# Weight-part stores moved from SyncE's queue to GpSimd's, and the weight-sum batches regrouped from 5, 6, 5 to 4, 6, 6

## What is computed

```
for l in range(DEPTH):
    h = _rmsnorm(x, norm_gain[l])
    proj = jnp.einsum('bsd,de->bse', h, w_in[l])               # 2048 x 4352
    q, k, v, g_attn, x_rnn, g_rnn = jnp.split(proj, splits, axis=-1)
    attn = _swa_sink_attention(q, k, v, sinks[l], cos, sin)
    xc = _causal_conv(x_rnn, conv_w[l], conv_b[l])
    rnn = _rg_lru(xc, w_rgate[l], b_rgate[l], w_igate[l], b_igate[l], lru_param[l])
    mixed = jnp.concatenate([attn * silu(g_attn), rnn * silu(g_rnn)], axis=-1)
    x = x + jnp.einsum('bse,ed->bsd', mixed, w_out[l])         # 2048 x 2048
return _rmsnorm(x, final_gain)
```

## Time and profile before

| | value |
|---|---|
| median of three runs | 2289.14 us |
| profiled execution | 2285.01 us, its span 2283.2 us |
| PE busy | 2275.7 us (100%) |
| DVE / ACT busy | 1568.7 us (69%) / 1315.0 us (58%) |
| POOL busy | 84.9 us (4%) |
| SP's queue q1 | 381.56 MB, 52.4% of the 16 DMA engines' span |
| POOL's queue q0 | 62.92 MB, 11.4% |
| HBM | 222 GB/s over the span |

### The profile page before, as it was taken

The page is one execution under the profiler, slowest core; times in us unless marked ns, Lnnn a source line. Parts: engine busy times, 40 slices in busy tenths (PEclk is TensorE's granted clock), DMA queues, the critical chain, the costliest instruction groups (busy, mean ns, idle before and its releaser), DMA issues.

```text
span 2283.2 us, 38210 instructions
## 1 busy us (share of the span) xinstructions
PE 2275.7 (100%) x14446; PEld 1939.6 (85%) x14446; DVE 1568.7 (69%) x2594; ACT 1315.0 (58%) x2536; POOL 84.9 (4%) x138
## 2 busy tenths in 40 slices
PE   9999999999999999999999999999999999999998
PEld 7888888899888888889988888888988888888898
DVE  7658778656546876856677777785568468778555
ACT  7558666444455867645565575663446557566444
POOL 1110000000111000000011100000000000000000
PEclk9999999999999999999999999999999999999999
DMA  8987777544788777644479866654545346666444
GB/s 255 258 234 259 238 241 239 156 135 142 212 245 233 252 235 240 214 142 138 139 233 267 263 206 203 214 190 146 141 130 170 99 134 196 208 202 196 140 134 153
DMA packets 173271, 447.01 MB, mean 196 GB/s; under 512 B 20768, under 2 KB 25120, under 8 KB 167200
## 3 DMA queue, kind: packets, MB, share of 16 engines
q1 hardware_dynamic: 165744, 381.56, 52.4%
q0 software_dynamic: 6912, 62.92, 11.4%
q10 hardware_dynamic: 432, 0.10, 0.0%
HBM read 365.85 MB, written 141.56 MB: 222 GB/s over the span
## 4 chain that ended last, share of the span: by engine, by line
PE 98%; DMA 1%; DVE 0%; ACT 0%; issue 0%; POOL 0%; ACTq 0%; DVEq 0%; POOLq 0%
PE proj L719 74%; PE proj L740 18%; PE ps_at L848 2%; PE ps_at L823 1%; PE ps_at L867 1%; PE proj L759 1%; DMA wall<-in_w 1%; PE proj L786 0%; ACT wcut L942 0%; PE ps_at L674 0%; DVE acc L1439 0%; ACT operand L979 0%; PE ps_at L801 0%; ACT sqr L1005 0%; DVE operand L1416 0%
## 5 line engine op out<-in xcount | busy, mean ns | idle before, releaser
L719 PE MATMUL proj<-operand,wcut 128*128 128x512 f32 x7512 | 1745.2, 391 | 0.3 <-DVE operand L1416 0.3
L719 PEld LDWEIGHTS proj<-operand,wcut 128*128 128x128 f32 x7512 | 1400.0, 188 | 297.4 <-issue 9.6
L1344 DVE TENSOR_TENSOR wcut<-wall,wcut 128x512 fp32r<-128x512 f32 x799 | 550.1, 688 | 537.1 <-ACT wcut L942 530.5
L942 ACT ACTIVATE wcut<-wall 128x512 fp32r<-128x512 f32 x798 | 501.9, 629 | 596.9 <-DMA wall<-in_w 322.8
L740 PEld LDWEIGHTS proj<-operand,wcut 128*128 128x128 f32 x1476 | 187.8, 191 | 6.5
L740 PE MATMUL proj<-operand,wcut 128*128 128x256 f32 x1476 | 189.8, 283 | 0.0
L740 PE MATMUL proj<-xsum_out,wcut 128*128 128x256 f32 x1104 | 136.8, 283 | 0.0
L740 PEld LDWEIGHTS proj<-xsum_out,wcut 128*128 128x128 f32 x1104 | 134.9, 192 | 0.6
L740 PE MATMUL proj<-xsum_in,wcut 128*128 128x256 f32 x864 | 111.8, 284 | 0.0
L740 PEld LDWEIGHTS proj<-xsum_in,wcut 128*128 128x128 f32 x864 | 107.9, 191 | 3.5 <-issue 1.7
L1048 ACT ACTIVATE gy<-proj 32x512 f32<-32x512 f32 x144 | 85.0, 590 | 14.9 <-PE proj L719 9.5
(11 more groups left out here) (186 smaller groups left out, 1733.6 us busy)
## 6 DMA issues: line engine op xcount, KB each, us to landing
wall<-in_w SPq DMA_DIRECT2D x494, 256.0 KB, 2.8
weight_cuts<-wcut SPq DMA_DIRECT2D x126, 512.0 KB, 3.9
wcut<-weight_cuts SPq DMA_DIRECT2D x126, 512.0 KB, 4.2
weight_sums<-in_blocks POOLq DMA_DIRECT2D x84, 512.0 KB, 6.6
wall<-weight_sums SPq DMA_DIRECT2D x164, 256.0 KB, 2.7
wall<-in_blocks SPq DMA_DIRECT2D x141, 256.0 KB, 2.8
weight_sums<-weight_sums POOLq DMA_DIRECT2D x28, 512.0 KB, 5.0
x<-in_xt SPq DMA_DIRECT2D x16, 512.0 KB, 3.7
```

The source lines that it names most:

```text
L719: last = pe.matmul(bank_of(l, 2 * g + m)[:, :], wcut[:, n % RING, a, c:c + P], operand[:, k, b, :], start=(i == 0 and k == 0), stop=(k == ...
L942: act.activation(wcut[:, u % RING, 0, :], wall[:, u % RING, 1, :], ACT.Copy).then_inc(w_hi, 1)
L1344: dve.tensor_tensor(wcut[:, u % RING, 1, :], wall[:, u % RING, 1, :], wcut[:, u % RING, 0, :].bitcast(F32), ALU.subtract).then_inc(w_lo, 1)
```

## The change

The 126 stores leave SP's loop. POOL issues them, 63 at a time, in a new function `store_parts(l)`: for each stored unit of layer l it waits on `w_lo` and issues the same 512 KB store. It calls this at the two turns of `OPENS`, after the closing addition of S4 and before the wait for PE. `OPENS` moves one turn forward: batches 0 to 3 come first, then the stores of layer 0; from unit 220 batches 4 to 9, then the stores of layer 1; from slot 4 of (h 1, l 0) batches 10 to 15.

```diff
-OPENS = {5: (0, 1, 1), 11: (1, 0, 4)}
+OPENS = {4: (0, 1, 1), 10: (1, 0, 4)}
...
                                 w_load(u + RING)
-                            if u + 2 in STORED:
-
-                                sp_.wait_ge(w_lo, SPLIT_NO[u + 2])
-                                sp_.dma_start(cuts[KEYS.index(key_of(l, *UNIT[u + 2][2:]))],
-                                              wcut[:, (u + 2) % RING, :, :].rearrange("p a c -> p (a c)").bitcast(F32)
-                                              ).then_inc(cut_out[(u + 2) % RING], 16)
...
+            def store_parts(l):
+
+                for n in STORED:
+                    if UNIT[n][1] == l:
+                        pool.wait_ge(w_lo, SPLIT_NO[n])
+                        pool.dma_start(cuts[KEYS.index(key_of(*UNIT[n][1:]))],
+                                       wcut[:, n % RING, :, :].rearrange("p a c -> p (a c)").bitcast(F32)
+                                       ).then_inc(cut_out[n % RING], 16)
+
             pool.wait_ge(unit_done, START_SUMS)
...
                 if n in OPENS:
                     pool.wait_ge(built[S4], 32 * n - 16)
                     add(S4, n - 1, A12)
+                    store_parts(list(OPENS).index(n))
                     pool.wait_ge(unit_done, at_unit(*OPENS[n]))
```

## The result

The changed kernel takes 2314.8 us, the median of five runs (2313.8 to 2317.0), against 2291.3 us (2285.3 to 2292.8) for the kernel before: a ratio of 1.0105 with an interval of 1.0092 to 1.0118, 23.5 us slower. (The median of the kernel before is now that of five runs, 2.2 us above that of the three known when the forecast was made.) The forecast was 13.5 us slower, 2302.6 us; the sign was right, the time lies above the range of 2293 to 2313.

A forecast was written before the change was run, and what follows sets the result against it. The prediction took PE, busy 2275.7 of 2283.2 us, as the bound, through matmul count and pitch. One 13.5 us loss in layer 1, all other terms nothing, on the median 2289.1 gave 2302.6 us, range 2293 to 2313.

The forecast's parts named there:

- What bounds the kernel: Whole kernel: PE's matmul number and pitch set the end, whatever the DMA share; at most 1.8 us of stalls removable.
- stores off SP: SP's queue loses 126 issues (54 us) and loads start earlier; PE doesn't wait for loads, so costed at nothing.
- stores on POOL in steady state: POOL gains 126 issues, 65 to 97 us in all, and keeps up three times over: costed at nothing.
- Layer 0: POOL is free at about 144, SP issued the first store at 163.68: 20 us to spare, cost nothing.
- Layer 1, steps 1 to 7: POOL reaches layer 1's stores at 752.0, unit 280's load lands late, PE stops ahead of `scores`: loss 13.5 us.
- The quiet of step 6: Layer 1, from about 739: SP's loads stand queued, so the DMA engines carry POOL's chain alone.
- The clock: PE's stop of 11.7 us may slow `scores` and unit 279: 2.1 us more, nothing added, 2 kept for the range.
- The third stretch, "Nothing": Batches 10 to 15: one half-size batch more, some 24 us, first consumer 138 units behind the start; costed at nothing.
- lost lead behind the gate: Rival: after layer 1's gate, ACT's and DVE's lost lead costs further stops, 2 to 5 us: 2306 us, chance 0.10.
- Slow stores through GpSimd: Rival: GpSimd's stores are slow in themselves, landing up to 11.6 us after issue; loss 20 us, 2309 us, chance 0.13.

The follow-up runs named there:

- p4543: Changed kernel with batches 4, 5, 4, 3, the last three behind a third wait at slot 1 of (h 1, l 1): 1.0010 against the kernel before.
- sp4543: Batches 4, 5, 4, 3 as in p4543, but with the stores left on SP: 1.0006 against the kernel before.
- p457: Changed kernel with batches 4, 5, 7, one less ahead of layer 1's stores and one more behind: 1.0036 against the kernel before.
- q3: Changed kernel with only a quarter of each addition in the third stretch (batches 10 to 15): 1.0056 against the kernel before.
- p475: Changed kernel with batches 4, 7, 5, one more ahead of layer 1's stores: 1.0155 against the kernel before.
- q23w: As q23, but POOL also waits for the end of unit 277 ahead of layer 1's stores: 1.0032 against the kernel before.
- q23: Changed kernel with only a quarter of each addition in batches 4 to 15, copies whole: 0.9976 against the kernel before.
- sp466: Kernel before with only the batches regrouped to 4, 6, 6, stores left on SP: 1.0055 against the kernel before.
- p466early: Changed kernel, batches 4, 6, 6, with the second stretch opened earlier, at slot 130 of (h 0, l 0): 1.0083 against the kernel before.
- p4552: Changed kernel with batches 4, 5, 5, 2, the last two from slot 24 of (h 1, l 1): 1.0023 against the kernel before.
- sp565late: Kernel before (stores on SP, batches 5, 6, 5) with the third stretch opened at slot 12 instead of 4 of (h 1, l 0): 1.0025.

## Why the prediction was right and where it failed

- *What bounds the kernel; stores off SP; stores on POOL in steady state*: right. SP's wait for stores to land, outside the stop, almost vanished (from 113.2 us in 105 waits to 23.5 in 4, of which 21.0 are the stop), and PE got nothing from it: p4543 and sp4543 are level.
- *Layer 0*: right. POOL was free at 143.6 and waited 14 us for the first part; no stop.
- *Layer 1, steps 1 to 7*: the mechanism was right in each link, the sizes were short. POOL came at 748.5, not 752.0 (the turns up to the sixth ended 4.6 us ahead, 1.0 of it the earlier start; the sixth took 27.4 us, forecast 26; the closing copy 4.3, forecast 4.4). The quiet of step 6 is there: the DMA share from 745 to 750 was 0.36, before 0.81. The store landed 7.4 us after its issue, not 5.0, behind the addition on the same queue. The load took 5.7 us to the moment ACT could use it, not 3.4, with four stores beside it. ACT began the part of 280 at 761.74 against the 760.4 forecast; from there to the gate 9.1 us instead of 8.0. Since everything ahead of this lies 1.0 us earlier than in the kernel before, that makes 17.0 instead of 13.5. With the full sums in layer 1, POOL in time (p457), at 748.5 (changed), 753.1 (q3) and 769.6 (p475) gives a loss of 0, 17.0, 20.5 and 34.9 us; q23w, with light sums and at 748.3, gives 13.4.
- *The clock*: the 2 us that the sum left out were largely there. The windows of the changed kernel, PEclk third from the end:

```profile
750.00:760.00 10.00, 0.04 (x1) 0.00 (x0) 0.00 (x0) 0.00 (x0) 1.25 (x3) 0.66 0.95 301
760.00:764.00 4.00, 0.00 (x0) 0.00 (x0) 1.56 (x3) 2.14 (x5) 0.53 (x1) 0.50 0.94 360
...
770.00:780.00 10.00, 10.00 (x44) 8.20 (x43) 9.18 (x18) 7.55 (x12) 1.60 (x3) 0.98 0.46 156
```

  `scores` took 1.99 us instead of 1.10 and unit 279 5.00 instead of 3.06, so PE came to the gate without waiting there: the term that the sum left at nothing was part of the loss. By what the Trainium skill states in "TensorE: Matmul & The Clock Gate", Part 1 (throttled is the default, activity releases it), the clock comes back by itself once PE works; the window behind 770, at 0.98, agrees.
- *The third stretch, "Nothing"*: this is the step that failed. It asked whether the sums would be in time for their first reader, unit 579, and they were. It didn't ask what the shifted batches run beside. In slots 30 to 55 of (h 1, l 0) the stores of x, the half-width units and the first ready-made parts share the DMA engines, at 0.88 already in the kernel before. The first section of the prediction read a pitch that doesn't depend on the DMA share and went on to "PE doesn't wait for loads"; here PE waited, through ACT and DVE, for single loads and a store of x that landed 11 to 14 us after their issue. The term measured 13.7 us in the changed kernel against the short execution of the kernel before; q3 removed it and left the rest. Against a usual execution it is less: p4543 and sp4543, level with the kernel before by their runs, show 7.6 and 5.8 us by the same measure. Of the 12.2 us between the forecast 2302.6 and the measured 2314.8, 2.2 are the median of the kernel before and 3.5 the first stop; the 6.5 that remain are an estimate of what the third stretch cost in the runs.
- *The rivals*: lost lead behind the gate wasn't seen (no wait between 771 and the third stretch). Slow stores through GpSimd, with the Trainium skill's rule on descriptors written by software ("DMA: Bandwidth & Descriptors", the section on SWDGE, HWDGE and iDMA) behind it: the 126 stores cost POOL 0.53 us each and landed in 3.9 us in the median, as SP's did before (at most 10.8 against 7.0), and p457 lost nothing in their layer. In these runs the rule's effect doesn't show; whether VectorE was in such a mode beside them no row tells.

By the medians the loss is 23.5 us where the spans give 29.7. The profiled execution before lies 6 us under the median of its kernel, that of the changed kernel at it. q23 is 4.7 us faster than the median of the kernel before without any stop of that one's profile to remove. That most runs of the kernel before lose some 5 us in its own full stretches is likely from this, but its profile doesn't show it.

What stays open: why the second loss is 13.7 us in the changed kernel, 6.7 in sp466 and 7.8 in p466early with the same six batches. The last store of x landed in 14.0, 9.7 and 8.3 us there, which fits, but how the bursts of POOL, the stores of x and the loads fall on each other differs between them, and no run held that fixed. Nor did a run take only the stores of x away, or only the half-size batch's place: that a whole batch in the place of the half one is what makes the transfers late is likely from p4552 and sp565late, not shown.

## What to carry to other kernels

When work is moved onto a queue, read at what time that queue is free and what its wait stands ahead of: the loss is the lateness, through every engine that works in order behind one load. A chain of DMAs that feeds nobody in a hurry can still cost where the DMA engines are near full: look along its whole length, not only at its end and its first reader, for the loads and stores beside it that another engine waits for, and compare the longest landing, not the median, with the lead. Moving such a chain, or changing the order of its large and small pieces, is a change too, even where its bytes stay the same. A DMA share of 0.5 isn't room for a second stream; here a chain of copies and additions took it to 0.94.

## What the runs showed of the hardware

- Stores of 512 KB from the core's memory to DRAM landed in 3.9 us in the median from GpSimd's queue (changed kernel, at most 10.8) as from SyncE's (before, at most 7.0), and cost GpSimd 0.53 us of issue each, with VectorE 68% busy.
- After 14 us without a matmul the granted clock was 0.50, and the next 1.10 us of `scores` took 1.99 us; it was at 0.98 in the window from 770 to 780, which begins 6 us behind PE's restart.
- The DMA engines' share stood at 0.87 to 0.94 with 247 to 270 GB/s in the windows shown in which PE was stopped beside the sums, but also at 0.88 with 266 GB/s in one in which it wasn't. The median landing of a 256 KB load was 6.2 us in the third stretch of the changed kernel, 5.4 in the kernel before and 3.8 with lighter sums (q3).
- In that stretch one 1 MB store of x landed in 5.3 us in the kernel before and in 13.4 to 14.0 us in four kernels in which PE stopped behind it for 2.1 to 5.7 us.
